# Moving the rounding of layer 0's projection weights from GpSimd to ACT in a one-core encoder step

## The chip, the cores and the metric

The kernel runs as one program on one core of a Trainium2 chip. The metric is device time in microseconds (us), from the start of the program to its end. A measured time is the median of several runs; a profile is one further execution, taken by the hardware profiler.

The core has a matrix engine (PE, with its weight loads listed apart as PEld), a vector engine (DVE), an activation engine (ACT), GpSimd (POOL) and a queue engine (SP) that issues transfers from HBM to on-chip SBUF. Each engine runs its own instructions strictly in the written order, and waits on semaphores that other engines raise.

## What is computed

One inference step of a two-layer streaming encoder, in float32, for 1024 prompt rows and 64 sample rows. The part that matters here is layer 0's differential attention: eight heads, each with its own 128 columns of Q, K and V weights.

```python
qkv = h @ w_qkv
q, k, v = jnp.split(qkv, [QA, 2 * QA], axis=-1)
...
s = jnp.einsum('bhqmd,bhkmd->mbhqk', q2, k2).astype(jnp.float32) * (DK_A ** -0.5)
s = s + t5_bias(qpos, kpos, table)[None, None]
mask = (kpos[None, :] // CHUNK) <= (qpos[:, None] // CHUNK)
s = jnp.where(mask, s, NEG)
p = jax.nn.softmax(s, axis=-1)
a = p[0] - lam * p[1]
return jnp.einsum('bhqk,bhkd->bhqd', a.astype(v.dtype), v)
```

The sample rows also attend to 512 cached keys and values per head. After layer 0's attention come a gated feed-forward block, a per-layer embedding, layer 1's attention, a second feed-forward block and a second embedding; the change doesn't touch them.

## The kernel before

**High and low parts.** To keep float32 accuracy, a large product is made of three products of rounded (float32r) operands: high by high, high by low, low by high (L911 to L913). So each weight chunk needs a high part (the chunk rounded) and a low part (the chunk less its high part).

**Layer 0's pipeline.** Attention is a loop of 72 steps, n = 9 h + t: head h, row tile t of 0 to 8. A row tile has 128 rows; tiles 0 to 7 attend to t + 1 blocks of 128 keys, tile 8 (the sample rows) to 512 cached keys and 64 new ones. In step n PE turns the probabilities of step n-2 (L1014), makes the scores of step n (L1063, bias L1071), runs the first half of one projection job, multiplies the probabilities of step n-2 by the values (L1090), turns one group of keys, values or cached keys (L1014), turns the output of step n-3 (L1014), and runs the job's second half. The two PSUM banks for turned blocks are used alternately, so a turn waits until the block two turns back has been copied out (`turn_a`, `bank_kept`).

**Projection jobs.** A job is one of K, Q or V for one of three row segments (384, 384 and 320 rows). In t = 3, 4 and 5 PE runs the last segments of K, Q and V of this head, in t = 6, 7 and 8 the first segments of Q, K and V of the next head. So the next head's Q weights are wanted in t = 6, K in t = 7, V in t = 8.

**The weight chunks.** All three chunks of the next head come through one buffer, `qkv_raw` (t_109 in the built program). SP loads a chunk (`qkv_chunk`, L466) when the previous chunk's low part has been made (`qkv_split`). POOL makes both parts in `split_qkv`: it waits for the load and for the last job that reads the old chunk, then rounds (L756, into `qkv_hi`, t_117 to t_119 for K, Q, V) and subtracts (L758, into `qkv_lo`, t_120 to t_122). In POOL's order this is done for K, Q, V in t = 4, 5 and 6 of heads 0 to 6; in between and behind stand the low part of the keys (L765), the masking and splitting of the bias (L770 to L776) and the splitting of the attention output (L790, L792). Head 7 has no next head, so in its tiles 4 to 6 POOL makes no weight parts.

**The other engines in a tile.** ACT copies the turned probabilities (L1470), makes the exponentials (L1478), the scale of an output (L1485 to L1489), in t = 5 the high part of the cached keys (L1514), and last copies the result of the step's job (L1498 and L1502 for K, L1504 for Q, L1508 for V). DVE scales an output (L1891), takes the maxima of the scores (L1862), then a reciprocal (L1872), a ratio (L1874, 128x1), the difference of the two probability maps (L1877), the copy of the output (L1885), in t = 5 the low part of the cached keys (L1909) or else a copy of turned keys or values (L1916), the turned output (L1901), and for Q its low part (L1923). L1874 and L1877 have both tensor inputs in SBUF; L1862, L1885, L1909, L1916, L1901 and L1923 read PSUM.

In the feed-forward blocks of the same kernel ACT already rounds weight chunks of this size (L1582) and POOL subtracts (L728).

Of the kernel before, what the change touches and what calls it, by code (L numbers as in the profile page):

```python
# [21 lines left out]
ALU = mybir.AluOpType  # L22
ACT = mybir.ActivationFunctionType
AX = mybir.AxisListType

P = 128
# [8 lines left out]
HA, DVA = 8, 128  # L35
# [9 lines left out]
CHUNK = 1024  # L45
# [55 lines left out]
def job_at(n):  # L101


    h, t = divmod(n, 9)
    kind, s = AT_STEP[t]
    head = h + (t >= 6)
    return (kind, head, s) if head < HA else None


def job_number(kind, h, s):  # L110


    if h == 0 and s == 0:
        return "KQV".index(kind)
    n = AT_STEP.index((kind, s))
    return 3 + 9 * (h - (n >= 6)) + n
# [84 lines left out]
def program(nc, x_prompt, x_sample, p_prompt, p_sample, cache_a_k, cache_a_v, cache_b_k, cache_b_v,  # L201
# [6 lines left out]
    with ctx:  # L208
# [4 lines left out]
        def place(word, shape, dt=F32):  # L213
            names[0] += 1
            return nc.alloc_sbuf_tensor_at(f"t{names[0]}", shape, dt, offset=base + 4 * word).ap()
# [27 lines left out]
        zero = small[:, 26:27]  # L243
# [41 lines left out]
        qkv_raw = place(S0 + 13312, [P, CHUNK])  # L285
# [5 lines left out]
        qkv_hi = [place(W0 + 2 * CHUNK * kind, [P, CHUNK], F32R) for kind in range(3)]  # L291
# [59 lines left out]
        def sem(name):  # L351
            return ctx.enter_context(nc.semaphore(name))
# [12 lines left out]
        q_high, qkv_kept = sem("q_high"), sem("qkv_kept")  # L365
        k_high, k_low = sem("k_high"), sem("k_low")
        qkv_loaded, qkv_round, qkv_split, job_done = sem("qkv_loaded"), sem("qkv_round"), sem("qkv_split"), sem("job_done")
        k_rawed, v_rawed, ktok_kept, v_kept = sem("k_rawed"), sem("v_rawed"), sem("ktok_kept"), sem("v_kept")
        kc_loaded, kc_high, kc_low, vc_loaded = sem("kc_loaded"), sem("kc_high"), sem("kc_low"), sem("vc_loaded")
        bias_loaded, bias_masked, bias_round, bias_split = sem("bias_loaded"), sem("bias_masked"), sem("bias_round"), sem("bias_split")  # L370
# [325 lines left out]
        def _(pool):  # L696
# [53 lines left out]
            def split_qkv(kind, h):  # L750

                j = 3 * h + kind
                pool.wait_ge(qkv_loaded, 16 * (j + 1))
                if h:
                    pool.wait_ge(job_done, job_number("KQV"[kind], h - 1, 2) + 1)
                pool.tensor_tensor(qkv_hi[kind], qkv_raw, zero.broadcast_to([P, CHUNK]), ALU.add).then_inc(qkv_round, 1)  # L756
                pool.wait_ge(qkv_round, j + 1)
                pool.tensor_tensor(qkv_lo[kind], qkv_raw, qkv_hi[kind].bitcast(F32), ALU.subtract).then_inc(qkv_split, 1)  # L758

            def keys_rest(h, s):  # L760
# [33 lines left out]
            for kind in range(3):  # L794
                split_qkv(kind, 0)
            split_bias(0)
            keys_rest(0, 0)
            for n in range(TILES_A + 4):
                h, t = divmod(n, 9)
                if t == 0 and h:  # L800
                    split_output_a(h - 1, 1)
                if t == 3 and h:
                    split_output_a(h - 1, 2)
                job = job_at(n)
                if h < HA and job is not None and job[0] == "K":
                    keys_rest(job[1], job[2])
                if h < HA - 1 and 4 <= t <= 6:
                    split_qkv(t - 4, h + 1)
                if h < HA and t == 6:
                    split_output_a(h, 0)  # L810
                if h < HA - 1 and t == 8:
                    split_bias(h + 1)
# [95 lines left out]
        def _(pe):  # L908
# [119 lines left out]
            def probabilities_a(n):  # L1028

                pe.wait_ge(diff_done, n + 1)  # L1030
                for g, blocks in enumerate(groups_of("A", n % 9)):
                    turn_a("P", first_turn_a(n) + g, [p_a[n % 2][:, 0, c:c + 128] for c, _, _ in blocks])
# [6 lines left out]
            def scores_a(n):  # L1039
# [26 lines left out]
                for m in range(2):  # L1066
                    for c0, c1, _, _, _ in pieces:
                        b0 = max(c0, first)
                        if b0 < c1:
                            for part in (bias_hi, bias_lo):  # L1070
                                last = pe.matmul(psf[:, 1024 * m + b0:1024 * m + c1], ident_r[:, :], part[:, b0 + o:c1 + o],  # L1071
                                                 start=False, stop=part is bias_lo, skip_group_check=True)
                    last.then_inc(s_done, 1)
# [308 lines left out]
        def _(act):  # L1382
# [78 lines left out]
            def probabilities_kept(n):  # L1461

                for g, blocks in enumerate(groups_of("A", n % 9)):
                    k = first_turn_a(n) + g
                    i = SLOT_A["P", k]
                    w = 128 * len(blocks)
                    act.wait_ge(t_done, i + 1)
                    if k >= 2:
                        act.wait_ge(pv_done, k - 1)
                    act.activation(aT[:, k % 2, 0:w], ps[:, 4 + i % 2, 0:w], ACT.Copy).then_inc(t_high, 1)  # L1470

            def exponentials_a(n, m):

                t = n % 9
                w = 128 * (t + 1) if t < 8 else PAST + TS
                col = 2 * (n % 2) + m
                act.wait_ge(max_done, 2 * n + m + 1)
                act.activation(p_a[n % 2][:, m, 0:w], psf[:, 1024 * m:1024 * m + w], ACT.Exp,  # L1478
                               bias=negmax[:, col:col + 1], accum_out=zsum[:, col:col + 1]).then_inc(exp_done, 1)

            def output_scale(n):

                c, b = 2 * (n % 4), n % 2
                act.wait_ge(o_done, n + 1)
                act.activation(osq, otok[b], ACT.Square, scale=rz[:, c:c + 1], accum_out=ssq[:, b:b + 1]).then_inc(osq_done, 1)  # L1485
                act.wait_ge(osq_done, n + 1)
                act.activation(orstd[:, b:b + 1], ssq[:, b:b + 1], ACT.Ln, bias=eps_col).then_inc(oln_done, 1)
                act.wait_ge(oln_done, n + 1)
                act.activation(orstd[:, b:b + 1], orstd[:, b:b + 1], ACT.Exp, scale=-0.5).then_inc(orstd_done, 1)  # L1489

            def job_kept(kind, h, s):

                a, w = SEGS[s]
                j, i = job_number(kind, h, s), 3 * h + s
                src = ps[:, j if j < 3 else 7, 0:w]
                act.wait_ge(job_done, j + 1)
                if kind == "K":
                    act.activation(k_hi[:, a:a + w], src, ACT.Copy).then_inc(k_high, 1)  # L1498
                    if i:
                        act.wait_ge(k_low, i)  # L1500
                        act.wait_ge(t_done, SLOT_A["K", i - 1] + 1)
                    act.activation(k_raw[:, 0:w], src, ACT.Copy).then_inc(k_rawed, 1)  # L1502
                elif kind == "Q":
                    act.activation(q_hi[:, a:a + w], src, ACT.Copy, scale=0.125).then_inc(q_high, 1)  # L1504
                else:
                    if i:
                        act.wait_ge(t_done, SLOT_A["V", i - 1] + 1)
                    act.activation(v_raw[:, 0:w], src, ACT.Copy).then_inc(v_rawed, 1)  # L1508

            def cached_keys_high(h):  # L1510

                i = SLOT_A["C", h]
                act.wait_ge(t_done, i + 1)
                act.activation(kc_hi, ps[:, 4 + i % 2, 0:PAST], ACT.Copy).then_inc(kc_high, 1)  # L1514
# [40 lines left out]
            for n in range(TILES_A + 3):  # L1555
                if 2 <= n < TILES_A + 2:
                    probabilities_kept(n - 2)
                if n < TILES_A:
                    exponentials_a(n, 0)
                    exponentials_a(n, 1)  # L1560
                if 2 <= n < TILES_A + 2:
                    output_scale(n - 2)
                if n < TILES_A:
                    if n % 9 == 5:
                        cached_keys_high(n // 9)
                    if job_at(n) is not None:
                        job_kept(*job_at(n))

            def ffn(l):
                c0, g0 = at[f"F{l}"]  # L1570
# [727 lines left out]
```

## Time and profile before

| | |
|---|---|
| time, median of 3 runs | 3357.88 us (3357.17 to 3358.34) |
| the profiled execution's own time | 3362.7 us |
| its span, first to last instruction | 3360.9 us |
| PE busy | 3129.2 us, 93% |
| DVE busy | 2023.5 us, 60% |
| ACT busy | 1103.7 us, 33% |
| POOL busy | 1033.2 us, 31% |
| mean granted TensorE clock | 0.968 of full |

The chain of waits that ended last is PE for 79% of the span, DVE for 11%, ACT for 3%; "issue" (6%) is time in which an engine waited for nothing that the profile shows. Layer 0's attention loop lies between about 73 and 697 us of the span.

How to read it: "busy" counts an engine's own instructions. Successive matmuls overlap in the record, so PE's busy time is not a measure of work done. What an engine waited for is printed behind an instruction in square brackets: the idle time before it, and the instruction that released it. The granted clock is given as a share of 2.4 GHz; 0.5 is 1.2 GHz.

### The profile page before, as it was taken

To read this page: it belongs to the slowest core of one execution; us is meant where nothing else is said; L and a number is where in the kernel's file an instruction comes from. 1 tells how busy PE (TensorE), PEld (TensorE's weight loads), DVE (VectorE), ACT (ScalarE), POOL (GpSimd) and SP (SyncE) were. 2 spreads that over 40 slices of the span, in tenths; PEclk is the share of its full clock that TensorE was granted. 3 is DMA by queue.
4 is the path that set the end of the run, shared out by engine and by line. 5 is a ranking of instruction groups with operands and counts; after the bars stand their busy time and mean duration, and the time that the engine had idled before them with its cause. 6 is when DMAs were issued, how large, how long until landed. Compare 5 with 4: busy or idle time off the path is not lost.

```text
span 3360.9 us, 50403 instructions
## 1 busy us (share of the span) xinstructions
PE 3129.2 (93%) x19213; PEld 2997.5 (89%) x19213; DVE 2023.5 (60%) x3097; ACT 1103.7 (33%) x2347; POOL 1033.2 (31%) x622
## 2 busy tenths in 40 slices
PE   6999998988999999999988899989899999999997
PEld 4888887887999999999987788879799999999997
DVE  6555555425665566666766777772666666656775
ACT  4444444412222222222422466660322222222242
POOL 2222323132222222222342677773122222222231
PEclk7999999989999999999998999999999999999998
DMA  3111122131111111111103212131111111111111
GB/s 117 53 55 61 54 62 63 48 122 38 39 50 40 44 44 45 44 45 55 43 26 91 60 56 59 53 124 38 32 45 45 44 45 44 45 45 44 51 39 59
DMA packets 248174, 182.21 MB, mean 54 GB/s; under 512 B 26949, under 2 KB 227605, under 8 KB 247829
## 3 DMA queue, kind: packets, MB, share of 16 engines
q1 hardware_dynamic: 232952, 163.53, 16.0%
q10 hardware_dynamic: 15004, 15.54, 1.4%
q8 instruction: 166, 2.72, 0.3%
q14 instruction: 52, 0.42, 0.0%
HBM read 142.54 MB, written 36.50 MB: 53 GB/s over the span
## 4 chain that ended last, share of the span: by engine, by line
PE 79%; DVE 11%; issue 6%; ACT 3%; DMA 1%; POOL 0%; DVEq 0%; ACTq 0%; SPq 0%; POOLq 0%
PE ps L911 22%; PE ps L913 21%; PE ps L912 21%; PE ps L1063 2%; PE ps L1201 2%; PE ps L1014 2%; PE ps L1090 2%; PE ps L1071 2%; PE ps L997 2%; DVE t L1812 1%; DVE t L1939 1%; DVE t L1799 1%; ACT t L1478 1%; ACT t L1534 1%; DVE t L1783 1%
## 5 line engine op out<-in xcount | busy, mean ns | idle before, releaser
L911 PE MATMUL ps<-t,t 128*128 128x384 f32 (+1 forms) x4920 | 1646.6, 335 | 51.1 <-DVE t L1799 11.7
L913 PE MATMUL ps<-t,t 128*128 128x384 f32 (+1 forms) x4920 | 1616.9, 329 | 0.0
L912 PE MATMUL ps<-t,t 128*128 128x384 f32 (+1 forms) x4920 | 1616.2, 328 | 0.0
L911 PEld LDWEIGHTS ps<-t,t 128*128 128x128 f32 x4920 | 933.1, 190 | 89.0 <-DVE t L1799 31.6
L912 PEld LDWEIGHTS ps<-t,t 128*128 128x128 f32 x4920 | 933.8, 190 | 0.4 <-issue 0.4
L913 PEld LDWEIGHTS ps<-t,t 128*128 128x128 f32 x4920 | 932.2, 189 | 0.0
L728 POOL TENSOR_TENSOR t<-t,t 128x1024 fp32r<-128x1024 f32 x181 | 473.7, 2618 | 1265.6 <-ACT t L1582 1262.2
L1773 DVE TENSOR_TENSOR t<-t,ps 128x384 f32<-128x384 f32 x528 | 260.6, 526 | 147.0 <-PE ps L913 144.9
L2018 DVE TENSOR_SCALAR t<-t 128x2 f32 (+1 forms) x88 | 16.9, 192 | 438.6 <-ACT t L1608 438.6
L1582 ACT ACTIVATE t<-t 128x1024 fp32r<-128x1024 f32 x130 | 138.0, 1061 | 413.8 <-PE ps L913 413.8
L1596 ACT ACTIVATE t<-ps 128x384 f32<-128x384 f32 x176 | 86.6, 493 | 502.7 <-PE ps L913 502.7
L722 POOL TENSOR_TENSOR t<-t,t 128x1024 fp32r<-128x1024 f32 x51 | 105.1, 2060 | 292.4 <-PE ps L913 291.8
L864 POOL TENSOR_TENSOR t<-t,t 128x128 f32<-128x128 f32 (+5 forms) x144 | 162.2, 1147 | 91.0 <-DVE t L2217 89.6
L1862 DVE TENSOR_REDUCE t<-ps 128x1 f32<-128x128 f32 (+5 forms) x144 | 102.8, 754 | 119.9 <-PE ps L1071 119.7
L2027 DVE SCALAR_TENSOR_TENSOR t<-t,t,t 128x1090 f32<-128x1090 f32 x88 | 165.5, 1881 | 9.0 <-DVE t L2024 0.3
L2024 DVE TENSOR_SCALAR t<-t,t 128x1090 f32<-128x1090 f32 x88 | 161.8, 1839 | 1.7
L1939 DVE TENSOR_TENSOR t<-ps,t 128x512 fp32r<-128x512 f32 (+1 forms) x184 | 115.6, 632 | 68.4 <-ACT t L1534 66.0
L1014 PE MATMUL ps<-t,t 128*128 128x128 f32 x576 | 93.1, 286 | 60.2 <-DVE t L1909 38.7
L1478 ACT ACTIVATE t<-ps,t 128x128 f32<-128x128 f32 (+5 forms) x144 | 105.7, 739 | 121.6 <-DVE t L1862 121.6
L1395 ACT ACTIVATE t<-t 128x1088 f32<-128x1088 f32 x56 | 62.3, 1112 | 240.4 <-DVE t L1986 184.5
L1201 PE MATMUL ps<-t,t 128*128 128x256 f32 (+1 forms) x656 | 119.5, 299 | 20.3 <-DVE t L1957 12.9
L997 PE MATMUL ps<-t,t 128*128 128x128 f32 x700 | 110.2, 276 | 26.0 <-DVE t L2137 22.0
(157 smaller groups left out, 3509.0 us busy)
## 6 DMA issues: line engine op xcount, KB each, us to landing
t<-in_w_ffn_in SPq DMA_DIRECT2D x88, 512.0 KB, 3.8
t<-in_w_ffn_out SPq DMA_DIRECT2D x44, 512.0 KB, 3.4
t<-in_w_qkv_a SPq DMA_DIRECT2D x24, 512.0 KB, 3.9
t<-in_w_ple_gate SPq DMA_DIRECT2D x16, 512.0 KB, 3.8
out<-t SPq DMA_DIRECT2D x32, 192.0 KB, 2.1
t<-in_x_prompt ACTq DMA_DIRECT2D x8, 512.0 KB, 7.3
t<-in_w_o_a SPq DMA_DIRECT2D x8, 512.0 KB, 4.0
t<-in_w_q_b SPq DMA_DIRECT2D x8, 512.0 KB, 4.7
```

Of the source, the lines that this page charges most:

```text
L728: pool.tensor_tensor(w_lo[slot][:, :], w_raw[slot][:, :], w_hi[slot][:, :].bitcast(F32), ALU.subtract).then_inc(w_split, 1)
L864: pool.tensor_tensor(probs, probs, rz[:, c + m:c + m + 1].broadcast_to([P, w]), ALU.mult).then_inc(scaled, 1)
L911: pe.matmul(out, a_hi, b_hi, start=start, stop=False, skip_group_check=True)
L912: pe.matmul(out, a_hi, b_lo, start=False, stop=False, skip_group_check=True)
L913: return pe.matmul(out, a_lo, b_hi, start=False, stop=stop, skip_group_check=True)
L997: m = pe.transpose(ps[:, bank, 128 * b:128 * b + rows], src, ident[0:rows, 0:rows])
L1014: m = pe.transpose(ps[:, 4 + i % 2, 128 * b:128 * b + 128], src, ident[:, :])
L1201: mm = pe.matmul(ps[:, 6, 0:256], v_both[r:P, vi, :], part[r:P, k % 2, 256 * b:256 * b + 256], start=g == 0 and b == 0 and part is bT_hi, ...
L1773: dve.tensor_tensor(xs, xs, ps[:, 8 - banks + j % banks, 0:w], ALU.add).then_inc(add_done, 1)
L1939: dve.tensor_tensor(bT_lo[:, k % 2, 0:w], ps[:, 4 + k % 2, 0:w], bT_hi[:, k % 2, 0:w].bitcast(F32), ALU.subtract).then_inc(t_free, 1)
L2024: dve.tensor_scalar(dst, ub[:, 2:T + 4], col(88), col(132), ALU.mult, ALU.add).then_inc(conv_step, 1)
L2027: dve.scalar_tensor_tensor(dst, ub[:, 1:T + 3], col(44), dst, ALU.mult, ALU.add).then_inc(conv_step, 1)
```

## The change

In heads 1 to 7, ACT now makes the high part (a copy with rounding into `qkv_hi`, new function `qkv_weights_high`, new semaphore `qkv_high`), at the very end of its steps t = 4, 5 and 6 of the head before, and takes over the two waits: for the load, and for the last job that reads the old chunk. POOL waits for ACT's copy, and only subtracts. The chunks of head 0 are made as before. SP, PE and DVE have the same instructions in the same order.

```diff
             def split_qkv(kind, h):
 
                 j = 3 * h + kind
-                pool.wait_ge(qkv_loaded, 16 * (j + 1))
                 if h:
-                    pool.wait_ge(job_done, job_number("KQV"[kind], h - 1, 2) + 1)
-                pool.tensor_tensor(qkv_hi[kind], qkv_raw, zero.broadcast_to([P, CHUNK]), ALU.add).then_inc(qkv_round, 1)
-                pool.wait_ge(qkv_round, j + 1)
+                    pool.wait_ge(qkv_high, j - 2)
+                else:
+                    pool.wait_ge(qkv_loaded, 16 * (j + 1))
+                    pool.tensor_tensor(qkv_hi[kind], qkv_raw, zero.broadcast_to([P, CHUNK]), ALU.add).then_inc(qkv_round, 1)
+                    pool.wait_ge(qkv_round, j + 1)
                 pool.tensor_tensor(qkv_lo[kind], qkv_raw, qkv_hi[kind].bitcast(F32), ALU.subtract).then_inc(qkv_split, 1)
...
+            def qkv_weights_high(kind, h):
+
+                j = 3 * h + kind
+                act.wait_ge(qkv_loaded, 16 * (j + 1))
+                act.wait_ge(job_done, job_number("KQV"[kind], h - 1, 2) + 1)
+                act.activation(qkv_hi[kind], qkv_raw, ACT.Copy).then_inc(qkv_high, 1)
+
...
                     if job_at(n) is not None:
                         job_kept(*job_at(n))
+                    if n < 9 * (HA - 1) and 4 <= n % 9 <= 6:
+                        qkv_weights_high(n % 9 - 4, n // 9 + 1)
```

ACT before, from the end of tile 4 of head 0 to the start of tile 6 (t_91 is `q_hi`, t_101 the turned probabilities, t_95 the high part of the cached keys, t_103 `v_raw`; ps is PSUM):

```order
L1504 ACTIVATE t_91<-ps 128x320 [waits job_done]
L1470 ACTIVATE t_101<-ps 128x512 [waits pv_done,t_done]
L1478 ACTIVATE t_111,t_66<-ps,t_66 128x768 [waits max_done] x2
L1485 ACTIVATE t_116,t_66<-t_68,t_66 128x128 [waits o_done]
L1487 ACTIVATE t_66<-t_66 128x1 [waits osq_done]
L1489 ACTIVATE t_66<-t_66 128x1 [waits oln_done]
L1514 ACTIVATE t_95<-ps 128x512 [waits t_done]
L1508 ACTIVATE t_103<-ps 128x320 [waits t_done,job_done]
L1470 ACTIVATE t_101<-ps 128x512 [waits pv_done,t_done]
```

ACT at the same place in the changed kernel, whose line numbers are some lines higher (L1506 is L1504 of before, L1472 is L1470, L1523 is L1514, L1510 is L1508):

```order
L1506 ACTIVATE t_91<-ps 128x320 [waits job_done]
L1517 ACTIVATE t_117<-t_109 128x1024 [waits job_done,qkv_loaded]
L1472 ACTIVATE t_101<-ps 128x512 [waits pv_done,t_done]
L1480 ACTIVATE t_111,t_66<-ps,t_66 128x768 [waits max_done] x2
L1487 ACTIVATE t_116,t_66<-t_68,t_66 128x128 [waits o_done]
L1489 ACTIVATE t_66<-t_66 128x1 [waits osq_done]
L1491 ACTIVATE t_66<-t_66 128x1 [waits oln_done]
L1523 ACTIVATE t_95<-ps 128x512 [waits t_done]
L1510 ACTIVATE t_103<-ps 128x320 [waits t_done,job_done]
L1517 ACTIVATE t_118<-t_109 128x1024 [waits job_done,qkv_loaded]
L1472 ACTIVATE t_101<-ps 128x512 [waits pv_done,t_done]
```

The new L1517 stands behind the copy of the job and ahead of the next step's copies of turned probabilities.

POOL before, from tile 3 to tile 6 of head 0 (t_94 is `k_lo`, t_109 `qkv_raw`; the last two rows split the output):

```order
L765 TENSOR_TENSOR t_94<-t_102,t_93 128x320 [waits k_rawed,k_high]
L756 TENSOR_TENSOR t_117<-t_109,t_66 128x1024 [waits job_done,qkv_loaded]
L758 TENSOR_TENSOR t_120<-t_109,t_117 128x1024 [waits qkv_round]
L756 TENSOR_TENSOR t_118<-t_109,t_66 128x1024 [waits job_done,qkv_loaded]
L758 TENSOR_TENSOR t_121<-t_109,t_118 128x1024 [waits qkv_round]
L756 TENSOR_TENSOR t_119<-t_109,t_66 128x1024 [waits job_done,qkv_loaded]
L758 TENSOR_TENSOR t_122<-t_109,t_119 128x1024 [waits qkv_round]
L790 TENSOR_TENSOR t_114<-t_112,t_66 128x384 [waits ot_kept]
L792 TENSOR_TENSOR t_113<-t_112,t_114 128x384 [waits oa_round]
```

POOL at the same place in the changed kernel (L767 is L765 of before, L760 is L758, L792 and L794 are L790 and L792):

```order
L767 TENSOR_TENSOR t_94<-t_102,t_93 128x320 [waits k_rawed,k_high]
L760 TENSOR_TENSOR t_120<-t_109,t_117 128x1024 [waits qkv_high]
L760 TENSOR_TENSOR t_121<-t_109,t_118 128x1024 [waits qkv_high]
L760 TENSOR_TENSOR t_122<-t_109,t_119 128x1024 [waits qkv_high]
L792 TENSOR_TENSOR t_114<-t_112,t_66 128x384 [waits ot_kept]
L794 TENSOR_TENSOR t_113<-t_112,t_114 128x384 [waits oa_round]
```

The three roundings are gone from POOL, and each subtraction now waits for ACT instead of for the load.

## Rows read from the trace of the kernel before

**Rows 1.** Waits, 90 to 660 us: who waited for whom, us, times, longest.

```profile
PE ps L1014 <- DVE t L1909: 36.9, 7, 5.4
PE ps L1014 <- DVE t L1916: 4.9, 7, 1.0
```

**Rows 2.** PE's timeline: start, us, engine, instruction, count, [idle before it <-releaser].

```profile
186.88 0.63 PE L1014 MATMUL ps<-t,t 128*128 128x128 f32 x4 [0.66 <-DVE t L1916]
...
199.62 1.30 PE L1014 MATMUL ps<-t,t 128*128 128x128 f32 x5 [5.24 <-DVE t L1909]
...
203.73 0.34 PE L911 MATMUL ps<-t,t 128*128 128x384 f32 x1
...
209.45 0.82 PE L1014 MATMUL ps<-t,t 128*128 128x128 f32 x6
...
651.21 0.60 PE L1014 MATMUL ps<-t,t 128*128 128x128 f32 x4
...
660.55 0.74 PE L1014 MATMUL ps<-t,t 128*128 128x128 f32 x5 [1.86 <-DVE t L1909]
...
663.22 1.27 PE L1090 MATMUL ps<-t,t 128*128 128x128 f32 x10
```

**Rows 3.** Timeline of POOL, tiles 4 and 5 of head 1.

```profile
182.75 2.38 POOL L758 TENSOR_TENSOR t<-t,t 128x1024 fp32r<-128x1024 f32 x1
191.84 1.89 POOL L756 TENSOR_TENSOR t<-t,t 128x1024 fp32r<-128x1024 f32 x1 [6.72 <-DMA t<-in_w_qkv_a]
193.81 2.35 POOL L758 TENSOR_TENSOR t<-t,t 128x1024 fp32r<-128x1024 f32 x1
```

**Rows 4.** Timeline of DVE: head 1, then head 7 from 652 us.

```profile
183.89 1.26 DVE L1874 SCALAR_TENSOR_TENSOR t<-t 128x1 f32<-128x1 f32 x1
...
192.33 1.42 DVE L1874 SCALAR_TENSOR_TENSOR t<-t 128x1 f32<-128x1 f32 x1
193.79 3.19 DVE L1877 SCALAR_TENSOR_TENSOR t<-t,t 128x768 f32<-128x768 f32 x1
...
216.16 0.22 DVE L1874 SCALAR_TENSOR_TENSOR t<-t 128x1 f32<-128x1 f32 x1
...
652.29 0.34 DVE L1891 TENSOR_SCALAR t<-t,t 128x128 f32<-128x128 f32 x1
653.53 1.82 DVE L1862 TENSOR_REDUCE t<-ps 128x1 f32<-128x768 f32 x2 [0.91 <-PE ps L1071]
...
656.63 0.22 DVE L1874 SCALAR_TENSOR_TENSOR t<-t 128x1 f32<-128x1 f32 x1
656.89 1.02 DVE L1877 SCALAR_TENSOR_TENSOR t<-t,t 128x768 f32<-128x768 f32 x1
...
659.72 0.69 DVE L1909 TENSOR_TENSOR t<-ps,t 128x512 fp32r<-128x512 f32 x1 [1.61 <-ACT t L1514]
...
660.58 0.34 DVE L1891 TENSOR_SCALAR t<-t,t 128x128 f32<-128x128 f32 x1
```

**Rows 5.** Two stretches: length, busy per engine, PEclk, DMA share, GB/s.

```profile
199.62:204.00 4.38, 4.38 (x23) 3.51 (x24) 0.68 (x3) 0.77 (x2) 4.09 (x2) 0.64 0.02 6
660.55:664.90 4.35, 4.35 (x35) 3.59 (x35) 2.09 (x4) 1.36 (x3) 1.87 (x2) 1.00 0.00 0
```

**Rows 6.** Line L1582: ns min/median/max, first and last start.

```profile
L1582 ACT ACTIVATE t<-t x130: 1043/1061/1075, 829.3 to 3159.1; 128x1024 fp32r<-128x1024 f32 x130
```

**Rows 7.** Timeline of ACT, end of tiles 4 and 5, head 7.

```profile
651.41 0.44 ACT L1504 ACTIVATE t<-ps 128x320 fp32r<-128x320 f32 x1
...
659.10 0.58 ACT L1514 ACTIVATE t<-ps 128x512 fp32r<-128x512 f32 x1
659.58 0.43 ACT L1508 ACTIVATE t<-ps 128x320 f32<-128x320 f32 x1
```

**Rows 8.** Timeline of SP, tile 5 of head 1: the cached keys' load.

```profile
192.54 0.37 SPq L473 DMA_DIRECT2D t<-in_cache_a_k  x1
```

**Rows 9.** Loads of these weight chunks, from issue to landing.

```profile
DMA to landing us min/median/max: 3.6/3.9/12.6
```

More of the change, by code:

```diff
@@ L367, in program @@
         qkv_loaded, qkv_round, qkv_split, job_done = sem("qkv_loaded"), sem("qkv_round"), sem("qkv_split"), sem("job_done")
+        qkv_high = sem("qkv_high")
         k_rawed, v_rawed, ktok_kept, v_kept = sem("k_rawed"), sem("v_rawed"), sem("ktok_kept"), sem("v_kept")
```

## The prediction, made before the result was known

> **What bounds the kernel now.** I read the waits of layer 0's attention loop first, then PE's timeline over one head, then, backwards from PE's waits, DVE, POOL and ACT. PE works almost without a gap there; what it loses stands in two places of each head that has a next one, that is in heads 0 to 6. The larger is at the start of tile 6: PE's first turn needs the bank of the cached keys, whose low part DVE makes late (L1909): 36.9 us in 7 waits [rows 1], 5.24 of them in head 1 [rows 2]. The smaller is at the start of tile 5 and waits for the turned keys' copy (L1916): 4.9 us in 7 [rows 1].
>
> Why is DVE late? In tile 5 of head 1 POOL rounds the Q chunk (L756) from 191.84 to 193.73 and subtracts (L758) from 193.81 to 196.16 [rows 3]. DVE's L1874, a 128x1 operation, starts at 192.33 and ends at 193.75, with L756; L1877 starts at 193.79 and ends at 196.98, 0.8 us behind L758 [rows 4]. Head 7 is the control: POOL makes no weight parts there, and the same two take 0.22 and 1.02 us [rows 4]. So POOL holds DVE up for 1.20 + 2.17 = 3.37 us. The next links follow in order: output copy (L1885), ACT's output scale and cached keys (L1485 to L1514), L1909, PE. In tile 4 the end of L758 (185.13) does the same to L1874 (183.89 + 1.26 = 185.15) [rows 3, 4], and PE waits 0.66 us at tile 5 [rows 2].
>
> The long wait costs once more behind itself: the granted clock is 0.64 over the next 4.4 us, partly at the 1.2 GHz level; after the 1.86 us that PE still waits in head 7 it is 1.00 [rows 5].
>
> **Rounding on POOL.** 21 L756 of 1.89 us go. POOL isn't what PE waits for, so this is worth only what DVE gets back. In head 7 tile 5 lasts 660.55 - 651.21 = 9.34 us against 199.62 - 186.88 = 12.74 in head 1 [rows 2]: 3.40 us, and that is the 3.37 that POOL held. Tile 4's subtraction leaves tile 4 as well (below): 0.66 us. If the wait at tile 6 shrinks to head 7's 1.86 us, I take the clock to stay up as there: the turns and scores at the start of tile 6 took 203.73 - 199.62 = 4.11 us in head 1, and 663.22 - 660.55 = 2.67 in head 7 [rows 2]: 1.44 us. Together 5.50 us for each head.
>
> This holds only if the subtraction, 2.4 us of POOL in a new place, meets none of L1874, L1877 or L1891 there, and if ACT and the loads are in time. I lay the new order over head 7's times, where DVE and ACT already run as they would.
>
> **Tile 5, the K chunk.** ACT's copy of the Q job ends at 651.41 + 0.44 = 651.85 [rows 7]. Then comes the new copy: the trace has the same operation, 1024 columns from SBUF, as L1582, 1.06 us [rows 6]. The K chunk has been loaded long before. It ends at 652.9; POOL subtracts from about 653.0 to 655.4. In that time DVE has L1862 alone, from 653.53, which reads PSUM; L1891 has started at 652.29, and L1874 comes at 656.63 [rows 4]. So nothing is held up. Behind the new copy on ACT is queued L1470, the turned probabilities; PE wants those behind the scores and half a job, about 4 us into the tile, so 1.06 us is hidden. ACT's exponentials can't start before L1862 has a maximum anyway.
>
> **The Q chunk, the only long chain.** SP issues its load when the K subtraction ends, 655.4; the median landing is 3.9 us [rows 9], 659.3. ACT comes to it behind L1508, at 659.58 + 0.43 = 660.0 [rows 7], so it finds it loaded, with 0.7 us to spare. Rounded by 661.07, subtracted from 661.2 to 663.5. DVE's L1891 has started at 660.58 [rows 4], before POOL. PE, though, wants both parts for the Q job of tile 6 at the end of the scores, 663.22 [rows 2], and waits about 0.31 us: a new wait, and the one term against the change. Its ends: nothing, if a link is 0.3 us shorter; and 1.6 us, if the load of the cached keys, which SP issues 192.54 - 186.88 = 5.7 us into tile 5 [rows 2, 8], thus with the Q load still under way, delays it by half its own time (256 KB beside 512 KB: 2.0 us, of which 0.7 is spare). I take 0.31, since the two overlap only in part.
>
> **Tile 7, the V chunk.** It is loaded from 663.5 to about 667.4, and ACT turns to it some 8.7 us into tile 6, at 669, so it doesn't wait. POOL subtracts from 1.8 to 4.2 us into tile 7 (counted as in tile 5). DVE's L1874 comes 216.16 - 209.45 = 6.7 us into it [rows 2, 4], which leaves 2.5 us for the pair that is queued behind on POOL (L790, L792). The V job is wanted in tile 8. Nothing is lost.
>
> **Sum.** 0.66 + 3.40 + 1.44 - 0.31 = 5.19 us for each head, times 7 = 36.3 us. The profiled execution took 3362.7 us and would take 3326.4; it stood 4.8 us above the median of the runs, 3357.9, so by the median 3321.6 us. The copy's 21 x 1.06 = 22 us on ACT cost nothing by this reckoning. Own range: with the Q wait at 1.6 us, 3.9 x 7 = 27 and 3331; with none and a little more at tile 5, 5.7 x 7 = 40 and 3318.
>
> **Rivals.**
> A. *POOL meets DVE in the new place.* In tile 5 L1891 starts 0.7 us before the subtraction, in tile 6 0.6 us before. If POOL came first in tile 5, L1891 would be held to 655.4 and L1862, due at 653.53 [rows 4], would start at 655.7, 2.2 us late. PE's wait at tile 6 is then 4.1 us; each head gains 5.19 - 2.2 = 3.0, or 1.5 if the clock falls too: 3337 to 3347. For it: margins under a microsecond. Against: both instructions follow the same end of L1504, L1891 behind one DVE operation, POOL behind ACT's 1.06 us. The Trainium skill, "SBUF — State Buffer", section "Who interferes with whom", states such a rule: a DVE instruction with two SBUF inputs, or in a two-port mode, and a GpSimd instruction that reads SBUF exclude each other, and whichever comes first holds the ports to its end; PSUM reads and ACT are free of it. By that rule the subtraction left on POOL still costs its full length wherever it starts first, and the sum stays 5.19 a head or becomes this rival's. The trace agrees: 3.19 us beside POOL, 1.02 without [rows 4].
> B. *It doesn't do what it seems to.* If POOL isn't what lengthens L1874 and L1877, the 5.24 us stay, and only the new order's 0.3 us a head is added: about 3360, within 0.2%. The agreement of ends to 0.02 us and head 7 speak against it.
> C. *Slower: ACT's wait for the Q load.* ACT now waits in order for a load that POOL used to wait for, with L1470 and L1478 of tile 6 queued behind, and PE behind these. With landing x us from issue, PE waits x - 4.6 + 0.3 us; from 4 us or so I count the clock's 1.44 as lost as well. The gain of 5.50 is used up at x = 8.4. At the longest landing of the trace, 12.6 us [rows 9], a head loses 8.3 + 1.44 - 5.5 = 4.2 us: 3387. Against: the median is 3.9, and the long ones would have to come in every head.
>
> **Chances.** Forecast 0.73, A 0.13, B 0.08, C 0.06. Range 3315 to 3347: forecast and A, 0.86, and a little below for terms that I undercount. A measurement of this kernel can tell about 0.2% (6.7 us) from no change: faster 0.86, same 0.08, slower 0.06.
>
> **What would show it.** L1874 and L1877 of tile 5 at 0.22 and 1.02 us in all heads; PE's wait at tile 6 near 1.9 us, the clock 1.00 behind it; no wait at the start of tile 5; a new wait of PE's Q job in tile 6 for the subtraction, some tenths; ACT's rounding in tile 6 not waiting for a load. It would be wrong if L1891 or L1862 of tile 5 or 6 moved back behind POOL (A), if L1877 stayed at 3.19 (B), or if ACT stood waiting for the load of Q or V (C).

## The result, and the profile after

The changed kernel took 3313.63 us in the median of 4 runs (3310.26 to 3316.07), the kernel before 3358.11 in the runs beside it: a ratio of 0.9866, 95% interval 0.9854 to 0.9878, or 44.5 us. The forecast was 3321.6 us with 3315 to 3347 as its range: the right direction and mechanism, but 1.4 us outside the range, on the fast side. Two later results of the same kernel gave 38.0 us (3318.16 against 3356.16; 0.9884, 0.9867 to 0.9900) and 41.3 us (3316.99 against 3358.24; 0.9873, 0.9858 to 0.9888). The mean of the three is 41.2 us.

In the changed kernel line numbers are higher: the ratio is L1885 (L1874 before), the difference L1888 (L1877), the output's scaling L1902 (L1891), the cached keys' low part L1920 (L1909), the maxima L1873 (L1862), PE's turns L1016 (L1014). The order that I laid over head 7 is there almost to the tenth. DVE's timeline in tiles 4 and 5 of head 1, to be read against [rows 4]:

```profile
175.72 0.22 DVE L1885 SCALAR_TENSOR_TENSOR t<-t 128x1 f32<-128x1 f32 x1
...
178.96 0.34 DVE L1902 TENSOR_SCALAR t<-t,t 128x128 f32<-128x128 f32 x1
180.21 1.82 DVE L1873 TENSOR_REDUCE t<-ps 128x1 f32<-128x768 f32 x2 [0.91 <-PE ps L1073]
...
183.31 0.22 DVE L1885 SCALAR_TENSOR_TENSOR t<-t 128x1 f32<-128x1 f32 x1
183.57 1.02 DVE L1888 SCALAR_TENSOR_TENSOR t<-t,t 128x768 f32<-128x768 f32 x1
...
187.26 0.34 DVE L1902 TENSOR_SCALAR t<-t,t 128x128 f32<-128x128 f32 x1
```

The ratio went from 1.26 and 1.42 to 0.22 us, the difference in tile 5 from 3.19 to 1.02, in all heads. ACT's and POOL's timelines of the same stretch, the K, Q and V chunk in turn:

```profile
178.42 1.05 ACT L1517 ACTIVATE t<-t 128x1024 fp32r<-128x1024 f32 x1
...
186.58 1.06 ACT L1517 ACTIVATE t<-t 128x1024 fp32r<-128x1024 f32 x1
...
196.57 1.05 ACT L1517 ACTIVATE t<-t 128x1024 fp32r<-128x1024 f32 x1
```

```profile
179.55 2.40 POOL L760 TENSOR_TENSOR t<-t,t 128x1024 fp32r<-128x1024 f32 x1 [6.90 <-ACT t L1517]
187.71 2.39 POOL L760 TENSOR_TENSOR t<-t,t 128x1024 fp32r<-128x1024 f32 x1 [5.76 <-ACT t L1517]
197.69 2.40 POOL L760 TENSOR_TENSOR t<-t,t 128x1024 fp32r<-128x1024 f32 x1 [7.60 <-ACT t L1517]
```

POOL subtracts from 179.55 to 181.95, where DVE has only its maxima, which read PSUM and take 1.82 us as in head 7 [rows 4]; L1902 started 0.6 us ahead of POOL in tile 5 and 0.45 us ahead in tile 6. ACT's copies show no wait in brackets: the loads had landed. PE at the start of tiles 5 and 6, against [rows 2], then the waits of PE from 90 to 640 us, against [rows 1]:

```profile
177.89 0.60 PE L1016 MATMUL ps<-t,t 128*128 128x128 f32 x4
...
187.23 0.74 PE L1016 MATMUL ps<-t,t 128*128 128x128 f32 x5 [1.87 <-DVE t L1920]
```

```profile
PE ps L1016 <- DVE t L1920: 15.0, 8, 1.9
...
PEld ps L913 <- POOL t L760: 1.5, 5, 0.3
```

The long wait is 1.87 us in all eight heads, as head 7 had foretold. The wait at tile 5 is gone (177.89 has no bracket), and the new wait of the Q job for POOL is 0.3 us.

**Where the 41 us are.** From PE's timeline I took the start of each tile's scores and summed the lengths of tiles 4, 5 and 6 over heads 0 to 6, in us, for every profiled execution:

| execution | tiles 4 | tiles 5 | tiles 6 | sum |
|---|---|---|---|---|
| before, first | 57.50 | 94.06 | 70.49 | 222.05 |
| before, second (before_again) | 57.52 | 93.45 | 70.49 | 221.46 |
| changed, first | 51.24 | 67.00 | 63.55 | 181.79 |
| changed, second (after_again) | 51.25 | 66.63 | 62.84 | 180.72 |
| changed, third (after_third) | 51.25 | 66.76 | 63.77 | 181.78 |

The means differ by 221.76 - 181.43 = 40.3 us. That is the gain, to 1 us, of the mean of the three results. The forecast had 36.3 us for these tiles.

### The profile page after: what moved, and what is told of

The parts are those of the page before. It is cut to its first block, busy times and chain, and to the rows that moved or that the text cites. A ratio compares the mean times of both kernels' runs of the same rounds, so it can differ in the third digit from the quotient of the medians.

```text
span 3308.5 us, 50403 instructions
## 1 busy us (share of the span) xinstructions
PE 3105.7 (94%) x19213; PEld 2978.8 (90%) x19213; DVE 1989.9 (60%) x3097; ACT 1123.2 (34%) x2368; POOL 994.4 (30%) x601
## 4 chain that ended last, share of the span: by engine, by line
PE 80%; DVE 10%; issue 5%; ACT 4%; POOL 1%; DMA 1%; DVEq 0%; ACTq 0%; SPq 0%; POOLq 0%
PE ps L913 22%; PE ps L915 22%; PE ps L914 22%; PE ps L1065 2%; PE ps L1203 2%; PE ps L1092 2%; PE ps L1016 2%; PE ps L999 2%; PE ps L1073 1%; DVE t L1823 1%; DVE t L1950 1%; DVE t L1810 1%; ACT t L1543 1%; DVE t L1794 1%; DVE t L1956 1%
## 5 line engine op out<-in xcount | busy, mean ns | idle before, releaser
L1873 DVE TENSOR_REDUCE t<-ps 128x1 f32<-128x128 f32 (+5 forms) x144 | 102.8, 754 | 110.1 <-PE ps L1073 109.9
L999 PE MATMUL ps<-t,t 128*128 128x128 f32 x700 | 110.2, 276 | 26.7 <-DVE t L2148 22.6
L1543 ACT ACTIVATE t<-ps 128x512 fp32r<-128x512 f32 (+1 forms) x184 | 101.3, 551 | 93.9 <-PE ps L999 90.6
```

The costliest lines, as they stand in the source:

```text
L999: m = pe.transpose(ps[:, bank, 128 * b:128 * b + rows], src, ident[0:rows, 0:rows])
```

## The experiments

**Three executions of the changed kernel, two of the kernel before.** No edit; they tell what is the change and what is scatter.

> The changed kernel once more, for a second profiled execution of it. Open from the first result: the gain was 44.5 us by the medians, I forecast 36.3. In the first pair of profiled executions the tiles 4 to 6 of heads 0 to 6 are 40.3 us shorter together, and some 11 us of the difference lie outside layer 0's attention, where the programs are the same. Theory (scatter): what lies outside is scatter between executions, in the granted clock mostly; then this execution has the same tiles 4 to 6 within 2 us in sum, but its stages outside differ from the first execution's by several us, and the median stays at 3312 to 3316. Rival (a gain outside): the change makes later stages faster too, by where they fall against the clock; then the stages outside are again some 8 to 11 us shorter than in every execution of the kernel before.

> The kernel before once more, for a second profiled execution of it. Theory: the wait of PE at tile 6 is again 5.1 to 5.4 us in heads 0 to 6, and the granted clock falls behind it in each head, for a time that differs from head to head: tile 6 takes 9.3 to 10.7 us, near 10.1 in the mean of the seven, where I had read one head with 9.35. Rival: tile 6 takes some 9.35 us in most heads, and the first execution had unusually long low stretches; then the clock isn't the term that I made too small.

> The changed kernel a third time. The first two results gave 44.5 and 38.0 us under the kernel before, where the tiles 4 to 6 of the first seven heads are 40.5 us shorter in the mean of two profiled executions of each. If what goes beyond these tiles is scatter between chips and executions, the gain is again 36 to 46 us, and tiles 4 to 6 sum to 181 us within 2. If there is a steady gain outside them, it stays above 43 us.

The sums of the table hold within 1.1 us, while the result moved from 44.5 to 38.0 and 41.3 us. after_again's median of 3318.16 us lies above the 3312 to 3316 expected of it; before_again took 3360.40 us in its single run, and PE's wait at tile 6 was 5.00 to 5.38 us there, where 5.1 to 5.4 was expected.

In the first pair of executions the programs' common stages outside layer 0's attention differed by some 11 us. The first feed-forward block took 823.1, 826.0 and 827.4 us in the three executions of the changed kernel, 826.5 in both of the kernel before (from the first logarithm of one norm on ACT, L1408, to that of the next): that is scatter. Three later stages were shorter in all three changed executions than in both of before: the first embedding (132.9 to 133.1 against 134.4 us), the second feed-forward block (825.2 to 825.7 against 827.3) and the second embedding (127.9 to 128.2 against 129.4 and 129.5), some 4.5 us together. Steps of this size also lie between two executions of one program: both_first and both_first_again, below, take 132.9 and 134.4 us for the first embedding, 825.5 and 826.9 for the second feed-forward block. And the mean of the three results, 41.2 us, leaves 1 us for all that lies outside the tiles of the table. So scatter is the better supported of the two theories; two executions of the kernel before are too few to exclude a small gain outside.

The second execution of before also settles the clock. Six us from the start of tile 6 in heads 0 to 6 of the kernel before (first execution) and of the changed kernel (first four and last heads); the third number from the end of a row is the granted clock:

```profile
121.39:127.39 6.00, 6.00 (x25) 4.95 (x26) 1.76 (x4) 1.04 (x3) 5.59 (x4) 0.50 0.01 3
199.62:205.62 6.00, 6.00 (x32) 5.13 (x33) 2.30 (x4) 1.57 (x3) 5.63 (x4) 0.73 0.01 4
276.63:282.63 6.00, 6.00 (x28) 4.94 (x29) 1.76 (x4) 1.03 (x3) 5.49 (x4) 0.61 0.01 3
354.05:360.05 6.00, 6.00 (x26) 4.93 (x27) 1.76 (x4) 1.04 (x3) 5.52 (x4) 0.52 0.00 0
432.13:438.13 6.00, 6.00 (x25) 4.93 (x26) 1.76 (x4) 1.04 (x3) 5.55 (x4) 0.50 0.00 0
510.40:516.40 6.00, 6.00 (x33) 5.11 (x34) 2.36 (x4) 1.64 (x3) 5.40 (x4) 0.75 0.00 0
587.43:593.43 6.00, 6.00 (x29) 4.94 (x30) 1.76 (x4) 1.04 (x3) 5.57 (x4) 0.63 0.00 0
```

```profile
114.58:120.58 6.00, 6.00 (x32) 4.95 (x33) 2.24 (x4) 1.92 (x4) 2.36 (x1) 0.72 0.31 89
187.23:193.23 6.00, 5.91 (x41) 5.15 (x42) 2.57 (x5) 3.27 (x7) 2.39 (x1) 1.00 0.31 88
258.76:264.76 6.00, 5.91 (x41) 5.14 (x42) 2.56 (x5) 3.26 (x7) 2.39 (x1) 1.00 0.31 89
330.31:336.31 6.00, 5.91 (x41) 5.15 (x42) 2.57 (x5) 3.27 (x7) 2.38 (x1) 1.00 0.29 87
...
544.91:550.91 6.00, 6.00 (x32) 4.94 (x33) 2.20 (x4) 1.95 (x4) 2.35 (x1) 0.72 0.29 86
```

Before, the clock falls behind every long wait, but for a different time: head 1, which I had read, has 0.73, the second highest of seven; in heads 0 and 4 the whole six us ran at the 1.2 GHz level. In the second execution tile 6 takes 9.28 to 10.59 us, 10.07 in the mean, and 10.07 in the mean of the first, where head 1 had 9.35. After, it falls in two heads of seven even behind 1.87 us (in one in the second execution, in two in the third). And head 7 of the kernel before, from which I took that the clock stays up behind such a wait [rows 5], shows this only in its first execution. In the second the six us behind the same wait of 1.86 us have 0.72:

```profile
657.53:663.53 6.00, 5.88 (x35) 4.59 (x35) 2.24 (x4) 1.51 (x3) 1.86 (x2) 0.72 0.00 0
```

**POOL reading beside DVE.** The changed kernel with two more POOL additions:

```diff
...
+                if h < HA - 1 and t == 5:
+                    pool.wait_ge(exp_done, 2 * n + 2)
+                    pool.wait_ge(qkv_split, 3 * h + 4)
+                    for r in range(2):
+                        pool.tensor_tensor(spare, qkv_hi[0][:, 0:600].bitcast(F32), qkv_lo[0][:, 0:600].bitcast(F32), ALU.add).then_inc(spared, 1)
+                        pool.wait_ge(spared, 2 * h + r + 1)
                 if h < HA - 1 and 4 <= t <= 6:
                     split_qkv(t - 4, h + 1)
```

> The changed kernel, with two extra POOL additions of 600 columns (about 1.4 us each) that read the K chunk's parts from SBUF and write a spare tile, placed in tile 5 of heads 0 to 6 where ACT's exponentials end, so that they run beside DVE's ratio and difference. Nothing waits for them but POOL's own next subtraction. Theory (POOL's SBUF reads hold up DVE): the ratio takes about 1.3 us, the difference about 2.4 instead of 1.02, PE's wait at tile 6 grows from 1.87 to about 4.4 us, and with the clock's fall behind it the time is 18 to 31 us above the changed kernel: 3332 to 3345. Rival (DVE was slow for another cause, such as the load landing at that time): ratio and difference stay at 0.22 and 1.02 us, and the time stays within 2 us of the changed kernel's.

It took 3341.93 us, 23.8 above after_again on the same chip (ratio to before 0.9957, 0.9941 to 0.9974), within what was expected. POOL's, DVE's and PE's timelines, tile 5 of head 1 (L815 are the additions, L1893 the ratio, L1896 the difference):

```profile
187.16 3.02 POOL L815 TENSOR_TENSOR t<-t,t 128x600 f32<-128x600 f32 x2 [1.22 <-ACT t L1488]
```

```profile
187.31 1.34 DVE L1893 SCALAR_TENSOR_TENSOR t<-t 128x1 f32<-128x1 f32 x1
188.69 2.30 DVE L1896 SCALAR_TENSOR_TENSOR t<-t,t 128x768 f32<-128x768 f32 x1
```

```profile
193.64 0.74 PE L1024 MATMUL ps<-t,t 128*128 128x128 f32 x5 [4.27 <-DVE t L1928]
```

POOL's two additions end at 190.18, the difference at 190.99: again 0.8 us behind POOL. The granted clock over the six us behind PE's 4.27 us of waiting is 0.72. Two instructions that no result needs bring back 23 of the 40 us (tiles 4 to 6: 204.24).

**POOL writing beside DVE.** The same place, five fills instead of the additions:

```diff
...
+                if h < HA - 1 and t == 5:
+                    pool.wait_ge(exp_done, 2 * n + 2)
+                    for r in range(5):
+                        pool.memset(spare, 0.0).then_inc(spared, 1)
+                        pool.wait_ge(spared, 5 * h + r + 1)
```

> The same place, but five POOL fills of the spare tile, 600 columns each, that write SBUF and read nothing (0.5 to 0.6 us each, 2.5 to 3 us together). Theory (it is POOL's reading that excludes DVE's second SBUF input): ratio and difference stay at 0.22 and 1.02 us, PE's wait at 1.87 us, and the time within 2 us of the changed kernel's. Rival (any POOL instruction on SBUF holds DVE up): as with the reads, 15 to 30 us slower.

It took 3317.65 us, 0.5 us from after_again (0.9881, 0.9865 to 0.9898). POOL, then DVE, at the same place (L1892 the ratio, L1895 the difference):

```profile
186.81 3.22 POOL L814 MEMSET t<- 128x600 f32 x5 [1.20 <-ACT t L1487]
```

```profile
186.99 0.22 DVE L1892 SCALAR_TENSOR_TENSOR t<-t 128x1 f32<-128x1 f32 x1
187.24 1.02 DVE L1895 SCALAR_TENSOR_TENSOR t<-t,t 128x768 f32<-128x768 f32 x1
```

POOL is busy for 3.2 us over both, and neither takes longer; PE's wait at tile 6 stays at 1.87 us. So it isn't POOL's being busy, but its reading of SBUF, that holds up DVE's two-input instructions. That is what the Trainium skill, "SBUF — State Buffer", section "Who interferes with whom", states, that such an instruction contends with a GpSimd instruction that reads SBUF and not with one that only writes it; the two runs agree, 2.30 against 1.02 us.

**Who rounds, or when.** The kernel before, where POOL keeps the rounding and starts at the place where ACT rounds in the changed kernel:

```diff
                 j = 3 * h + kind
+                if h:
+                    pool.wait_ge(qkv_turn, j - 2)
                 pool.wait_ge(qkv_loaded, 16 * (j + 1))
                 if h:
...
+                    if n < 9 * (HA - 1) and 4 <= n % 9 <= 6:
+                        act.activation(spare[:, 0:1], zero, ACT.Copy).then_inc(qkv_turn, 1)
```

> The kernel before, in which POOL still makes both parts, but starts each chunk only when ACT has reached the place where the changed kernel rounds (a 128x1 copy on ACT tells it). It separates where POOL's work stands from who rounds. Theory (the place decides: POOL must not read SBUF while DVE makes ratio and difference): both at 0.22 and 1.02 us in tile 5; but POOL's 4.3 us now hold the output's scaling on DVE at the start of tile 5 and delay PE's wait by about 0.9 us (2.7 instead of 1.87), and the Q chunk is ready about 1.4 us later than PE wants it; a head gains 3.4 to 4 us of the changed kernel's 5.8: 24 to 28 us under the kernel before. Rival (ACT's rounding itself is the gain): within 5 us of the kernel before.

3325.37 us against 3359.31: 34 us under the kernel before (0.9907, 0.9890 to 0.9924), more than the 24 to 28 expected; tiles 4 to 6 sum to 190.02, 31.7 under before. DVE, then PE, in tiles 5 and 6 of head 1 (L1897 the output's scaling, L1883 the difference):

```profile
181.63 1.70 DVE L1897 TENSOR_SCALAR t<-t,t 128x128 f32<-128x128 f32 x1
...
186.34 0.22 DVE L1880 SCALAR_TENSOR_TENSOR t<-t 128x1 f32<-128x1 f32 x1
186.60 1.02 DVE L1883 SCALAR_TENSOR_TENSOR t<-t,t 128x768 f32<-128x768 f32 x1
```

```profile
190.26 0.74 PE L1018 MATMUL ps<-t,t 128*128 128x128 f32 x5 [2.23 <-DVE t L1915]
194.28 0.44 PE L915 MATMUL ps<-t,t 128*128 128x384 f32 x1 [1.21 <-POOL t L762]
```

Ratio and difference are free; what POOL now meets is the scaling, 1.70 instead of 0.34 us, of which 0.4 us reaches PE (2.23 instead of 1.87), and Q comes 1.21 us late where I had 1.4. So by these tiles four fifths of the gain (31.7 of 40.3) are the later place of POOL's work; ACT's rounding gives the rest: POOL, with the subtraction alone, starts behind the scaling and ends sooner.

**The clock by itself.** The kernel before with 28 matmuls of no use in PE's wait:

```diff
+                    if n % 9 == 6 and n < 9 * (HA - 1):
+                        pe.wait_ge(exp_done, 2 * n)
+                        for r in range(28):
+                            pe.matmul(psf[:, 0:384], ident_r[:, :], h_hi[:, r % KT, 0:384], start=True, stop=True,
+                                      skip_group_check=True)
                     if 0 <= u < TILES_A:
                         probabilities_a(u)
```

> The kernel before, with 28 matmuls of 384 columns without use, about 4.9 us, into a score bank that is free then, at the start of tile 6 of heads 0 to 6, where PE waits 5.2 us for the cached keys. They fill the wait and nothing else. Theory (the clock falls because PE stands still there): the granted clock behind the wait stays at 1.00, tile 6 and the start of it take 1.4 to 2.1 us less for each head: 10 to 15 us under the kernel before. Rival (the clock falls for another cause, or the matmuls delay the turns): within 4 us of the kernel before, or slower.

3347.84 us, 11.5 under the kernel before (0.9969, 0.9956 to 0.9981). PE's timeline at tile 6 of head 1 (L1136 are the added matmuls), and the stretches around it, with the granted clock third from the end:

```profile
192.65 5.02 PE L1136 MATMUL ps<-t,t 128*128 128x384 f32 x28
198.07 0.74 PE L1014 MATMUL ps<-t,t 128*128 128x128 f32 x5 [0.40 <-DVE t L1914]
198.74 1.50 PE L1063 MATMUL ps<-t,t 64*128 64x512 f32 x12
```

```profile
194.00:199.00 5.00, 4.60 (x29) 4.14 (x29) 2.83 (x5) 2.07 (x7) 1.15 (x2) 1.00 0.36 105
199.00:203.00 4.00, 4.00 (x30) 3.61 (x29) 2.09 (x2) 1.67 (x5) 3.92 (x3) 1.00 0.00 2
```

The wait is as long as ever, only filled, and the scores run in 1.50 us instead of 2.37; in all seven heads the clock is 1.00 over the six us behind it; tiles 5 and 6 together are 164.25 - 152.17 = 12.1 us shorter in the seven heads, 1.7 us each. So the low clock cost 1.7 us a head, and it is the standing still that brings it.

**A version that beats both.** The profile after shows two waits, 1.87 us of cached keys and 0.3 us of Q, and ACT idle in tile 5 ahead of the output's scale. First only the cached keys:

```diff
+                if n < TILES_A and n % 9 == 5:
+                    cached_keys_high(n // 9)
                 if 2 <= n < TILES_A + 2:
                     output_scale(n - 2)
                 if n < TILES_A:
-                    if n % 9 == 5:
-                        cached_keys_high(n // 9)
```

> The changed kernel, with ACT making the high part of the cached keys in tile 5 ahead of the output's scale instead of behind it. By my account of the chain, PE's remaining wait at tile 6 falls from 1.87 to about 0.1 us in all eight heads; but the Q chunk is then ready about 1.6 us after PE wants it, so seven heads give back 1.3 us each: 3 to 6 us under the changed kernel. Rival (the Q chunk isn't on the edge): 13 to 15 us under it.

3312.78 us (0.9867, 0.9850 to 0.9883). Tiles 4 to 6 sum to 178.13, 3.3 us under the changed kernel's mean; its waits:

```profile
PE ps L913 <- POOL t L760: 9.7, 7, 1.8
...
PE ps L1016 <- DVE t L1920: 1.4, 8, 0.2
```

The first wait went from 15.0 to 1.4 us, and the Q job's rose to 9.7: the Q chunk was next in line, as expected. Then Q earlier as well:

```diff
                 if n < TILES_A and n % 9 == 5:
                     cached_keys_high(n // 9)
+                    if n < 9 * (HA - 1):
+                        qkv_weights_high(1, n // 9 + 1)
...
-                    if n < 9 * (HA - 1) and 4 <= n % 9 <= 6:
-                        qkv_weights_high(n % 9 - 4, n // 9 + 1)
+                    if n < 9 * (HA - 1) and n % 9 in (3, 6):
+                        qkv_weights_high(0 if n % 9 == 3 else 2, n // 9 + 1)
...
-                store_keys_a(h, 2)
                 if h < HA - 1:
                     qkv_chunk(1, h + 1)
+                store_keys_a(h, 2)
+                if h < HA - 1:
                     load_cached_keys(h + 1)
```

> The same, and the Q chunk earlier as well: ACT rounds the K chunk at the end of tile 3, SP issues the Q load ahead of the store of the keys, and ACT rounds Q in tile 5 behind the cached keys, where it stands idle. By my account both the wait at tile 6 and the wait of the Q job go: 8 x 1.8 + 7 x 0.3 = 16 us under the changed kernel. Rival (DVE's output scaling, which POOL's Q subtraction then holds up, comes too late for tile 6): less than 8 us.

> The version with cached keys, K and Q earlier, beside the changed kernel on the same chip. From the profiles (tiles 4 to 6 of seven heads 164.9 against 181.3 us, and head 7 some 2 us): 15 to 19 us under the changed kernel.

3297.72 us (0.9821, 0.9805 to 0.9838), and again 3298.73 (0.9818, 0.9805 to 0.9832), there 18.3 us under the changed kernel on the same chip. Tiles 4 to 6 sum to 164.9 us in both. The Q job waits no more, though POOL's Q subtraction now holds DVE's output scaling in tile 6 to 1.56 us; of PE's waits at tile 6 this is left:

```profile
183.65 0.74 PE L1017 MATMUL ps<-t,t 128*128 128x128 f32 x5 [0.16 <-DVE t L1923]
```

## Why the prediction was right in kind and too small

- **POOL holds up DVE's ratio and difference: right.** 0.22 and 1.02 us after, 1.34 and 2.30 when only reads are put back, untouched by writes. Rival B falls.
- **Head 7 as the control: right for lengths and waits, lucky for the clock.** PE's wait fell from 36.9 / 7 = 5.27 to 1.87 us, the 3.40 that I had. But that the clock stays up behind such a wait held in five heads of seven (six in the second execution), and for head 7 itself in one of the two executions of before.
- **The moved subtraction meets nothing: right.** The margins ahead of the output's scaling were 0.6 and 0.45 us, near the 0.7 and 0.6 that I had; rival A didn't come, and pool_both_later shows what it looks like (1.70 us).
- **The Q chunk's load and the new wait: right.** ACT waited for no load (rival C falls), and the Q job waits 0.3 us for POOL, as reckoned.
- **Tile 4, 0.66 us: too small.** Tile 4 went from 8.17 to 7.32 us in six heads, 6.3 us in the seven, 0.89 each. The printed wait counts from the end of the last matmul's record, while matmuls that follow without a wait overlap in the records (those of this job, before, are 0.31 us long and start 0.15 us apart); the tile's length holds that too. 0.23 x 7 = 1.6 us.
- **The clock, 1.44 us: the step that failed.** I took it from head 1 alone, and head 1 has nearly the shortest low stretch of the seven: its 4.11 us of turns and scores at the start of tile 6 are 4.04 to 4.79 us in the seven heads. Tiles 5 and 6 together gained 164.25 - 130.18 = 34.1 us, 4.87 a head, where the terms 3.40 + 1.44 - 0.31 give 4.53: 0.34 x 7 = 2.4 us. As the 3.40 and the 0.31 came out as read, the clock's term measured 4.87 - 3.40 + 0.31 = 1.78 us instead of 1.44. The filled wait gives 1.7 us a head directly; the changed kernel's own low stretches, one or two heads in seven, are already taken off in the 4.87.
- **The range: too tight below.** 1.6 + 2.4 = 4.0 us of mis-sized terms put the centre at 3317.6, still inside the range. The other 4 us of the first result are not in the tiles that the change touches and didn't stay: the two further results, 3318.16 and 3316.99 us, lie inside. So that the sum was 4 us short is shown; that the first result fell outside the bound was partly chance. My lower bound allowed for neither the heads' spread nor the scatter of a median of four, whose runs lie 6 us apart.

## What to carry to other kernels

An engine that is off the critical path can still be what lengthens it: where GpSimd instructions read SBUF, look whether vector instructions beside them end together with them, and give the GpSimd work a place where the vector engine reads PSUM or waits. A stretch of the same program that lacks the suspect (here the last head) is a good control for lengths and waits, and a later chain can be laid over its times. A term such as the clock behind a wait must be read in all repetitions, and in a second execution, not in the one that happens to be open.

## What the runs showed that was not expected

A vector instruction of one element per partition paid the whole remaining length of the reading GpSimd instruction beside it (1.42 us instead of 0.22), as did the output's scaling, which takes one tensor and two columns (1.70 instead of 0.34). Five GpSimd fills of 128x600 took 3.22 us with their waits, 0.64 each. The granted clock fell behind some idle stretches of 1.87 us and not behind others of the same length in the same execution.
